# Mean subtraction on GpSimd, a turned memory map, two output tiles kept back, and stores on ScalarE's queue in an eight-core encoder step

## The reference

```python
def conv_mixer(a, hist, w, b, ng, nb):
    h = jnp.concatenate([hist.astype(a.dtype), a], axis=1)
    y = lax.conv_general_dilated(h, w[:, None, :], window_strides=(1,), padding='VALID', ...) + b   # depthwise, width 31
    y = jax.nn.silu(layernorm(y, ng, nb))          # over 2048 channels
    return y, h[:, -CONV_HIST:]

def sgu_mixer(u, v, ws, bs, ng, nb):
    vn = layernorm(v, ng, nb)
    ...
    s = jnp.einsum('hij,bnjhc->bnihc', wm, vc) + jnp.transpose(bs[:, :L])[:, :, None]   # wm: lower triangular, 128 x 128
    y = u * s.reshape(B, T, E)
    return y, vn[:, -L:]
```

## Time and profile before

| | |
|---|---|
| median of 3 runs | 3977.95 us (3621.7, 3977.95, 4221.78) |
| profiled execution | 3649.39 us |
| span of its slowest core (core 0) | 3647.8 us |
| spans of the eight cores | 3594.0 to 3647.8 us |
| busy: TensorE, VectorE, ScalarE, GpSimd | 94%, 72%, 39%, 21% of the span |

### The profile page before, as it was taken

The page is one execution under the profiler, slowest core; times in us unless marked ns, Lnnn a source line. Parts: engine busy times, 40 slices in busy tenths (PEclk is TensorE's granted clock), DMA queues, the critical chain, the costliest instruction groups (busy, mean ns, idle before and its releaser), DMA issues.

```text
span 3647.8 us, 58188 instructions; the slowest of 8 cores (3594.0 to 3647.8 us)
## 1 busy us (share of the span) xinstructions
PE 3439.8 (94%) x17838; PEld 1717.8 (47%) x18112; DVE 2628.1 (72%) x4357; ACT 1422.6 (39%) x2199; POOL 769.3 (21%) x1394
## 2 busy tenths in 40 slices
PE   7889999988999997899999999999999899999998
PEld 3334444544555553344454444444455444444554
DVE  6869998965778776977875545554555678888887
ACT  3334343423455554444553333343333233333332
POOL 2313332311434432000011111111111132121221
PEclk9999999999999998889999999999999999999999
DMA  7698878686666675768797556774675843333243
GB/s 137 139 245 199 195 176 181 168 216 152 113 137 135 124 186 183 234 194 262 235 284 209 153 161 189 208 192 163 190 224 181 273 155 131 111 113 107 95 135 123
DMA packets 394193, 639.03 MB, mean 175 GB/s; under 512 B 170824, under 2 KB 234824, under 8 KB 386592
## 3 DMA queue, kind: packets, MB, share of 16 engines
q0 software_dynamic: 75824, 311.43, 33.7%
q1 hardware_dynamic: 318064, 323.86, 29.7%
HBM read 564.26 MB, written 197.23 MB: 209 GB/s over the span
## 4 chain that ended last, share of the span: by engine, by line
PE 77%; DMA 7%; DVE 6%; issue 5%; SPq 2%; ACT 2%; POOL 0%; DVEq 0%; ACTq 0%; POOLq 0%
PE ps L659 47%; PE ps L791 19%; PE ps L1484 6%; DMA arena<-xin 2%; PE ps L1223 2%; DVE arena L741 1%; PE ps L853 1%; DMA hd<-arena 1%; DMA arena<-yd 1%; DMA arena<-sgrow 1%; PE ps L1554 1%; DVE arena L1393 1%; DVE arena L950 1%; DMA yd<-arena 1%; DMA arena<-wst 1%
## 5 line engine op out<-in xcount | busy, mean ns | idle before, releaser
L659 PE MATMUL ps<-arena 128*128 128x512 bf16 (+1 forms) x10196 | 2159.2, 365 | 55.6 <-DVE arena L1144 10.1
L659 PEld LDWEIGHTS ps<-arena 128*128 128x128 bf16 x10368 | 1011.3, 99 | 1056.0 <-issue 121.5
L791 PE MATMUL ps<-arena 128*128 128x512 bf16 (+1 forms) x4545 | 971.2, 366 | 35.6 <-DVE arena L1401 27.8
L791 PEld LDWEIGHTS ps<-arena 128*128 128x128 bf16 x4608 | 454.7, 99 | 513.0 <-issue 90.7
L616 POOL DMA_DIRECT2D arena<-wq x441 | 235.1, 534 | 1481.6 <-PE ps L791 704.9
L950 DVE TENSOR_TENSOR arena<-arena 128x526 f32<-128x526 f32 (+6 forms) x720 | 473.3, 663 | 67.7 <-ACT arena L930 32.0
L704 ACT ACTIVATE arena<-arena 128x512 bf16<-128x512 f32 (+1 forms) x360 | 211.4, 592 | 647.9 <-DVE arena L795 588.3
L795 DVE TENSOR_TENSOR arena<-ps,arena 128x512 f32<-128x512 f32 (+1 forms) x288 | 185.4, 644 | 158.4 <-PE ps L791 141.8
L716 DVE TENSOR_TENSOR arena<-arena 128x512 f32<-128x512 bf16 (+3 forms) x258 | 166.1, 644 | 140.2 <-ACT arena L704 139.8
L969 ACT ACTIVATE arena<-ps 128x512 f32<-128x512 f32 (+1 forms) x288 | 161.9, 562 | 227.7 <-PE ps L659 199.7
L1484 PE MATMUL ps<-arena 128*128 128x512 bf16 x1029 | 239.2, 382 | 7.3 <-DMA arena<-hd 5.9
(11 more groups left out here) (98 smaller groups left out, 2546.5 us busy)
## 6 DMA issues: line engine op xcount, KB each, us to landing
arena<-wq POOLq DMA_DIRECT2D x441, 512.0 KB, 5.8
wq<-wst POOLq DMA_DIRECT2D x88, 512.0 KB, 7.8
xs<-arena SPq DMA_DIRECT2D x144, 256.0 KB, 6.3
arena<-xs SPq DMA_DIRECT2D x144, 256.0 KB, 6.6
arena<-wst POOLq DMA_DIRECT2D x64, 512.0 KB, 8.0
arena<-hd SPq DMA_DIRECT2D x26, 1024.0 KB, 6.7
arena<-xin SPq DMA_DIRECT2D x96, 256.0 KB, 8.6
yd<-arena SPq DMA_DIRECT2D x96, 256.0 KB, 4.6
```

What stands on the lines that cost most here:

```text
L659: r = e.matmul(P[:, 0:T], lhsT=W[:, k * 256 + base:k * 256 + base + 128], rhs=H[:, k * st:k * st + T], start=(k == 0), stop=(k == 7))
L791: r = e.matmul(P[:, 0:T], lhsT=W[:, k * 128:(k + 1) * 128], rhs=ym[k].ap(BF16)[:, 0:T], start=(k == 0), stop=(k == 15))
```

## The change

- In `ln_post` the subtraction of the mean goes from VectorE to GpSimd, for all 144 tiles.
- In `layout` the areas of the conv back are turned around: its y tiles, LayerNorm rows and small tables lie first, its gate tiles `zs` and extra weight slots last; `t1` gets two other places. In `conv_back` the gate tiles of group 0 and group 1 get other sets of places.
- `conv_back` loads h of the spatial layer's group 0 at the start of its last group; `sgu_layer` takes it over.
- In `sgu_layer` six output tiles are taken out during the v loop instead of eight, and two after it.
- The stores L624 and L869 are issued on ScalarE instead of SyncE.
- In `conv_front` the output tiles of layer 0 are taken out one group step earlier.
- `ln_table` takes its PSUM tile from the pool of two (`pst`) instead of the pool of six (`ps`).

```diff
-        C_zs = offs(R + 52 * kb, 2048, 8)
-        C_y = offs(R + 68 * kb, 2048, 10)
-        C_ex = offs(R + 96 * kb, 4096, 4)
+        C_y = offs(R + 52 * kb, 2048, 10)
+        C_zs = offs(R + 84 * kb, 2048, 8)
+        C_ex = offs(R + 100 * kb, 4096, 4)
...
-        self.lnr = Pool(S, "lnr", 2048, offs(R + 88 * kb, 2048, 4))
-        self.dg = Pool(S, "dg", 1024, offs(R + 112 * kb, 1024, 2))
+        self.lnr = Pool(S, "lnr", 2048, offs(R + 72 * kb, 2048, 4))
+        self.dg = Pool(S, "dg", 1024, offs(R + 80 * kb, 1024, 2))
...
-        self.t1 = Pool(S, "t1", 1024, offs(R + 55 * kb, 1024, 3) + offs(b + 61 * kb, 1024, 2))
+        self.t1 = Pool(S, "t1", 1024, offs(R + 55 * kb, 1024, 3) + offs(b + 49 * kb, 1024, 2))
...
-                self.hold(lambda after: S.add("sp", lambda e: e.dma_start(out=dst, in_=t.ap(BF16)), reads=[t], writes=[("wq", name)],
-                                              cost=0.45, nbytes=128 * 4096, dk=t, after=after))
+                self.hold(lambda after: S.add("act", lambda e: e.dma_start(out=dst, in_=t.ap(BF16)), reads=[t], writes=[("wq", name)],
+                                              cost=0.3, nbytes=128 * 4096, dk=t, after=after))
...
-                "sp", lambda e: e.dma_start(out=dst, in_=wp[half].ap(BF16)), reads=[(wp[half], k) for k in range(8)],
+                "act", lambda e: e.dma_start(out=dst, in_=wp[half].ap(BF16)), reads=[(wp[half], k) for k in range(8)],
...
-                if ct == 0 and 1 <= i <= 4:
-                    self.pull(2)
-                if ct == 0 and i == 5:
+                if ct == 0 and i < 4:
+                    self.pull((2,2,2,2)[i])
+                if ct == 0 and i == 4:
                     self.drain()
...
-        p, acc = self.ps.tile(), self.acc
+        p, acc = self.pst.tile(), self.acc
...
-        S.add("dve", lambda e: e.tensor_tensor(out=y.ap()[:, 0:T], in0=y.ap()[:, 0:T], in1=m.ap()[:, 0:T], op=ALU.subtract),
-              reads=[y, m], writes=[y], cost=c_tt(T))
+        pool = True
+        S.add("pool" if pool else "dve", lambda e: e.tensor_tensor(out=y.ap()[:, 0:T], in0=y.ap()[:, 0:T], in1=m.ap()[:, 0:T], op=ALU.subtract),
+              reads=[y, m], writes=[y], cost=c_pool(T) if pool else c_tt(T))
...
-        ZB = list(range(12, 30))
+        Z0 = [list(range(4, 12)), list(range(20, 30))]
+        Z1 = list(range(4)) + list(range(12, 20))
...
-            z = self.zs.tile(ZB if g == 0 else ZA)
+            z = self.zs.tile(Z0[ct // 8] if g == 0 else Z1 if g == 1 and ct < 12 else ZA)
...
+            else:
+                hn = self.load_h(0)
...
-        h = self.load_h(0)
+        h = self.h_next
...
-                    if 2 * (it + 1) // nch > 2 * it // nch:
+                    if 6 * (it + 1) // (4 * nch) > 6 * it // (4 * nch):
                         self.pull()
...
+            self.pull(2)
             hn = self.load_h(g + 1) if g + 1 < NG else None
```

More of the change, by code:

```diff
@@ L538, in layout @@
         self.yp = Pool(S, "y", 2048, C_y)
-        self.lnr = Pool(S, "lnr", 2048, offs(R + 88 * kb, 2048, 4))
-        self.dg = Pool(S, "dg", 1024, offs(R + 112 * kb, 1024, 2))
-        self.lnt = Pool(S, "lnt", 1088, [R + 114 * kb])
-        self.lnw = Pool(S, "lnw", 544, [R + 114 * kb + 1088])
+        self.lnr = Pool(S, "lnr", 2048, offs(R + 72 * kb, 2048, 4))
+        self.dg = Pool(S, "dg", 1024, offs(R + 80 * kb, 1024, 2))
+        self.lnt = Pool(S, "lnt", 1088, [R + 82 * kb])
+        self.lnw = Pool(S, "lnw", 544, [R + 82 * kb + 1088])
         self.vr = Pool(S, "vr", 8192, D_vr)
@@ L1453, in conv_back @@
             self.add_out(1, g, ym, wn)
+        self.h_next = h
     def sgu_layer(self):
```

## The result

The changed kernel took 3670.22 us in the median (3660.83 at the least), the kernel before 3801.43 (3621.7 at the least) in runs beside it. The ratio of after to before is 1.0121, with a 95% interval of 1.007 to 1.0171: by the bound of 2% no difference, but by its interval slower. The forecast was 3618 us with a range of 3575 to 3690. The time lies in the range, but on the wrong side of no change: against an undisturbed execution of the kernel before (3626 us by the prediction) 8 us were to be gained, and some 40 were lost. Only two executions of the kernel before carry this ratio (3621.7 and 3624.92); in the five later series its medians are 3630 to 3640 us, and against those the profiled 3664.92 us is 0.7% to 1.0% more.

What follows compares the result with a forecast made beforehand. TensorE, 94% busy, was taken as the bound. From the profiled 3649.4 us, minus 14 (tiles), 5 (h), 7 (stores), 0 (map) and 2 (drain), plus 20 (subtraction), minus 23.2 (clock stretch) gave 3618 us; range 3575 to 3690.

Steps and rivals of the forecast that it cites:

- the 0.81 stretch: Conv back, cores 0 and 1: TensorE's granted clock of 0.81 in the profiled execution; counted as absent afterwards, 23.2 us less.
- Two tiles: Spatial layer: two output tiles put behind the v loop cover TensorE's nine waits for normalised v; gain 14 us.
- Early load of h: First spatial matmul: h asked for a whole group earlier removes its 5.91 us wait; gain 5 us.
- Stores: Layer 0: 24 weight stores leave SyncE's queue, 13 us gained at best, 6 charged to ScalarE; net gain 7 us.
- Map: Conv back's first two groups: gate tiles in other places change nothing; 0 us, bounds 10 gained and 5 lost.
- Drain: Conv front: output tiles taken out one step earlier shorten a 4.63 us stall on L741; gain 2 us.
- The subtraction: Conv back: GpSimd's subtraction excludes VectorE work with two SBUF inputs; loss 20 us, 12 in the first two groups, 8 later.
- this sum over a group: Later groups of 512 tokens: 58.5 us of excluding and unoverlapped work against TensorE's 55.2; 0 to 3.3 us lost in each.
- Rival 1: Conv back: GpSimd and VectorE run freely, 19 us gained instead of 20 lost; 3579 us, chance 0.17.
- Rival 2: Conv back: GpSimd starves and becomes the bound once a subtraction takes over 3.1 us; 3765 us, chance 0.10.
- Rival 3: Layer 0: the stores stop ScalarE's evictions, 20 us lost instead of 7 gained; 3645 us, chance 0.08.
- Rival 4: Conv back: the stretch at a clock of 0.81 comes again; 3641 us, chance 0.15.

Runs made afterwards that it cites:

- e4: The kernel before with only the spatial layer's order of work changed (two output tiles kept for after the v loop); ratio to before 0.9935.
- e14: The changed kernel with the subtraction on GpSimd only for tiles 8 to 15 of groups 2 to 8, otherwise on VectorE; ratio to before 0.9993.
- e15: The changed kernel with the subtraction on GpSimd only for tiles 0 to 7 of groups 2 to 8, otherwise on VectorE; ratio to before 1.0063.
- e2: The kernel before with only the subtraction of the mean moved to GpSimd; its two lowest executions took 3672.64 and 3679.57 us, no ratio.
- e6: The changed kernel with the subtraction back on VectorE, every other edit kept; 3625.13 us, ratio to before 0.9986.
- e3: The kernel before with only the weight stores L624 and L869 issued on ScalarE; 3633.82 us, ratio to before 1.0003.
- e8: The changed kernel with the subtraction back on VectorE and the stores back on SyncE; 3616.85 us, ratio to before 0.9947.
- e9: The changed kernel with the subtraction of every second tile on GpSimd, of the others on VectorE; ratio to before 1.0053.
- e12: The changed kernel with the subtraction on VectorE in groups 0 and 1 and on GpSimd in the later ones; 3660.07 us, ratio to before 1.0061.
- e7: The kernel before with only the memory map, the buffer sets and the PSUM tile of ln_table changed; 3632.45 us, ratio to before 0.9993.
- e5: The changed kernel with a GpSimd fill of a scratch buffer in place of the subtraction, the mean not subtracted; ratio to before 0.9941.

## Why the prediction was wrong

- **What bounds the kernel: right.** TensorE stayed at 94%; the losses found are waits of TensorE and its lower clock behind them. The base without the 0.81 stretch, 3649.4 - 23.2 = 3626, was right within 4 to 14 us: the medians of before are 3630 to 3640 in the later series, the lowest times 3621.7 to 3631.9, and its cores with that clock have 254 us in groups 2 to 5 where the others have 225.
- **Two tiles, gain 14: right in mechanism, a little low**: the nine waits are gone, with 15.6 us in the changed kernel and 20.1 in e4.
- **Early load of h, gain 5: wrong, about 0.** The 5.91 us were those of core 0; cores 1, 2 and 4 of the same trace waited there mostly for weights (0.7, 3.5 and 4.3 us). The sum named what is late next (weights) and still counted the gain.
- **Stores, gain 7: wrong size, 0 within 0.2%.** On core 2 the gain was 16.0 us and in the mean of the cores 9.0, where 11.1 to 13 were forecast; the cost was 15 to 16 where 6 was charged. The step that failed is the cover of 10 us by six PSUM tiles: it was set against 2 us of excess averaged over 22 us of ScalarE, while the issues come as one block of 15 us.
- **Map 0: right by its ratio. Drain, gain 2: none left.** Its own stall went as said (4.6 to 0.5 us), and a longer wait for a weight load took its place.
- **The subtraction, loss 20: mis-sized, 44.6.** In the first two groups 14.6 in place of 12: right. In the later groups 30.0 in place of 8, over the upper bound of 25; in the four of 512 tokens 4.7 us each, where at most 3.3 were allowed. The step that failed is this sum over a group: it added the work that excludes each other (58.5 us) and compared it with TensorE's 55.2, as if all of a group's slack were to be had where it is needed. The slack is elsewhere in the group: e14 puts half of the subtractions there and loses 2.6 us in four groups, e15 puts half of them at the normalizations and loses 19.5. A second step failed with it: from the copy of the earlier trace rows the prediction concluded that "VectorE pays nothing", and took its instructions at their old length, though it had noted that "whether VectorE also waits no run here shows yet". VectorE waits as well, and by more than it gave away (88.9 us against 61.6). The Trainium skill's rule ("SBUF — State Buffer", Who interferes with whom), as the prediction gave it, that the later one waits for the whole of the other, agrees for both sides where instructions alternate (0.74 becomes 1.75 us beside a subtraction of 1.71); it does not where GpSimd has several in a row, behind all of which VectorE's one instruction ended (4.33 and 7.89 us, in the last section). There the measurement decides.
- **Rivals.** Rival 1 (free running) fell by e2 and e6. Rival 2 (GpSimd starves at over 3.1 us) fell: 1523 ns in the mean, and no wait of TensorE for a weight load among those of groups 2 to 5. Rival 3's mechanism happened at 17.1 us (13.54 + 3.52) and was given back in e3; whether all of it is in the changed kernel, e6 against e8 leaves open. Rival 4 did not occur. That the time fell into the range at all is in part luck: the loss of the subtraction was over twice the term, and the range had room for it because it also allowed for the clock and the stores.

From 3618: 24.6 on the subtraction, 7 on the stores, 5 on h, 2 on the drain and -1.6 on the tiles give 3655. The lowest run is 3660.8 and the profiled one 3664.9, 6 to 10 us more, and the cause of these stays open. In the mean of the cores the changed kernel is 5.3 us later than before at the first band matmul (855.7 against 850.4) and takes 5.8 us longer from there to the first subtraction (583.7 against 577.9); but e6, e9, e12, e14 and e15, which differ from it in nothing but where the subtraction runs, reach that matmul at 852.1 to 861.6 us, and e3 and e7, which have the drain of before, take 583.2 and 586.0 us for the second part. Differences of this size come without an edit that would explain them.

## What to carry to other kernels

Before moving work from VectorE to GpSimd, count what both read from SBUF, and count it at the place where VectorE's result is waited for, not over the stage: a sum over a group can show slack, and one collision at its tightest point costs its delay in every group (4.7 us of some 56 here). If the move is wanted, choose the pieces by where they run (tiles 8 to 15 here), not by their number. Here even those gained nothing (0.9993, where e6 has 0.9986), since TensorE is the bound in those groups. And an instruction that only issues a transfer can hold its engine for microseconds (5.68 us for one store here); give it to the engine with the least urgent work behind it.

## What the runs showed of the hardware

- An operation of VectorE with two SBUF inputs (L741) took 0.74 us alone, 1.75 beside one subtraction of GpSimd, and 4.33 us through three of them in a row; GpSimd's of 512 columns took 1.26 alone and 1.71 beside it. Where GpSimd had several ready, its own kept 1.26 us and VectorE's one stood through all of them. In e14 (core 4) one square sum lasted through four subtractions, a weight load's issue and two more, and it had begun before all but the first:

```profile
1642.86 7.89 DVE L716 TENSOR_TENSOR arena<-arena 128x512 f32<-128x512 bf16 x1 [0.83 <-ACT arena L704]
...
1642.24 4.93 POOL L1392 TENSOR_TENSOR arena<-arena 128x512 f32<-128x512 f32 x4
1647.12 0.57 POOL L616 DMA_DIRECT2D arena<-wq  x1
1647.70 2.49 POOL L1392 TENSOR_TENSOR arena<-arena 128x512 f32<-128x512 f32 x2
```

- A GpSimd fill of 1.26 us, which only writes, left VectorE's operations at 0.685 us (e5). The reciprocal kept 3.34 us beside subtractions of 1.26 to 1.27, and the additions that read PSUM (L795) kept 0.68.
- In groups 2 to 5 one idle time of 3.2 to 3.8 us a group (3.81, 3.71, 3.20 and 3.45 on core 2) goes with a granted clock of 0.97 over the stretch in place of 1.00. Of the 4.7 us that a group is longer, 3.5 are the wait; the rest goes with the lower clock right behind it, where 15 matmuls take 4.97 us and 16 at the full clock take 3.62.
- Stores of 512 KB issued back to back cost ScalarE 0.4 to 1.2 us each at first and then 9.94 us for two and 5.68 for one, with the DMA engines at a share of 0.92; SyncE showed the like the earlier trace rows.
